# Loading half of the experts' late weight chunks through ScalarE's DMA queue

## The reference, cut to what matters

```python
def expert_ffn(xb, w1, b1, w2, b2):       # per expert: w1 [1024, 2048], w2 [1024, 1024]
    h = xb @ w1 + b1
    gate, up = h[:, :D_FF], h[:, D_FF:]
    gate = jnp.minimum(gate, SWIGLU_LIMIT)
    up = jnp.clip(up, -SWIGLU_LIMIT, SWIGLU_LIMIT)
    glu = gate * jax.nn.sigmoid(SWIGLU_ALPHA * gate)
    return ((up + 1.0) * glu) @ w2 + b2
```

## Time and profile before

| | us |
|---|---|
| median of 3 runs | 1476.92 |
| the profiled execution | 1473.57 |
| its span, as in the profile | 1471.8 |
| PE busy | 1367.5 (93%) |
| ACT busy | 233.6 (16%) |
| loads through the hardware queue q1 (SyncE), share of the 16 engines' time | 76.1% |
| granted TensorE clock, mean | 0.996 |

### The profile page before, as it was taken

One profiled execution on the slowest core, in us unless ns is written; L12 is line 12 of the kernel. 1 busy time (PEld: TensorE's weight loads), 2 busy tenths in 40 slices (PEclk: granted clock), 3 DMA queues, 4 the chain that ended last, 5 costly groups with the idle time before them and its releaser, 6 DMA issues.

```text
span 1471.8 us, 18292 instructions
## 1 busy us (share of the span) xinstructions
PE 1367.5 (93%) x7503; PEld 705.3 (48%) x7503; DVE 362.3 (25%) x671; ACT 233.6 (16%) x355; POOL 99.5 (7%) x167
## 2 busy tenths in 40 slices
PE   7999999999999989999889989899898898898987
PEld 6667668778888534433333233233332332332323
DVE  3224332532411242221212212212122122121222
ACT  1122232211000331111001111110011111100112
POOL 1022222220000210000000000000000000000000
PEclk9999999999999999999999999999999999999999
DMA  9787868775342459999999999999999999999995
GB/s 371 299 296 271 292 227 296 278 274 192 134 157 115 177 208 426 429 429 428 427 428 428 429 428 430 428 427 428 428 429 428 430 428 427 429 427 429 428 430 228
DMA packets 52321, 518.70 MB, mean 352 GB/s; under 512 B 6223, under 2 KB 6527, under 8 KB 19998
## 3 DMA queue, kind: packets, MB, share of 16 engines
q1 hardware_dynamic: 37418, 468.56, 76.1%
q0 software_dynamic: 12784, 45.34, 9.2%
q10 hardware_dynamic: 2084, 4.30, 0.8%
HBM read 496.55 MB, written 21.67 MB: 352 GB/s over the span
## 4 chain that ended last, share of the span: by engine, by line
DMA 53%; PE 43%; issue 1%; DVE 1%; ACT 1%; POOL 0%; SPq 0%; ACTq 0%; DVEq 0%; POOLq 0%
DMA ring<-in_w_pairs 46%; PE bank L1353 18%; PE bank L1644 11%; DMA out_ret_sample<-arena 5%; PE bank L1396 3%; PE bank L1683 2%; PE bank L1490 2%; PE bank L1593 1%; PE bank L1608 1%; PE bank L1455 1%; DMA k_kept<-arena 1%; PE bank L1444 0%; POOL arena L595 0%; DMA arena<-v_decode 0%; PE bank L1433 0%
## 5 line engine op out<-in xcount | busy, mean ns | idle before, releaser
L1644 PE MATMUL bank<-ring,arena 128*64 128x512 f32 x2048 | 461.0, 596 | 62.8 <-DMA ring<-in_w_pairs 61.3
L1353 PE MATMUL bank<-arena,ring 128*128 128x264 f32 x1536 | 349.5, 388 | 0.0
L1644 PEld LDWEIGHTS bank<-ring,arena 128*64 128x64 f32 x2048 | 141.4, 137 | 364.5 <-issue 273.3
L1353 PEld LDWEIGHTS bank<-arena,ring 128*128 128x128 f32 x1536 | 289.7, 190 | 53.2 <-issue 5.0
L1683 PE MATMUL bank<-ring,arena 128*64 128x512 f32 x1024 | 229.0, 595 | 11.5 <-DMA ring<-in_w_pairs 11.5
L1683 PEld LDWEIGHTS bank<-ring,arena 128*64 128x64 f32 x1024 | 70.9, 137 | 153.3 <-issue 124.9
L1305 DVE COPY arena<-bank 64x512 f32<-64x512 f32 x32 | 21.9, 684 | 237.5 <-PE bank L1683 237.5
L1283 DVE TENSOR_SCALAR arena<-bank 128x512 f32<-128x512 f32 x32 | 22.1, 692 | 231.8 <-PE bank L1644 231.8
L669 POOL CAST arena<-cst 128x128 bf16 x17 | 5.0, 296 | 907.9 <-PE bank L1672 907.9
L1608 PE MATMUL bank<-arena 128*128 128x512 f32 x136 | 62.9, 605 | 0.0
L1273 DVE TENSOR_TENSOR hs<-hs,bank 128x256 f32<-128x256 f32 x17 | 7.2, 421 | 223.7 <-PE bank L1604 223.7
(11 more groups left out here) (215 smaller groups left out, 850.3 us busy)
## 6 DMA issues: line engine op xcount, KB each, us to landing
ring<-in_w_pairs SPq DMA_DIRECT2D x192, 2048.0 KB, 24.4
ring<-in_w_mixer SPq DMA_DIRECT2D x60, 1024.0 KB, 9.8
arena<-in_state_ret POOLq DMA_DIRECT2D x32, 512.0 KB, 5.6
out_ret_sample<-arena POOLq DMA_DIRECT2D x32, 512.0 KB, 5.7
arena<-v_decode POOLq DMA_DIRECT2D x32, 256.0 KB, 8.4
out_ret_prompt<-arena ACTq DMA_DIRECT2D x4, 512.0 KB, 5.1
hx<-in_x_prompt SPq DMA_DIRECT2D x2, 512.0 KB, 3.7
v_kept<-arena ACTq DMA_DIRECT2D x2, 512.0 KB, 9.3
```

The source lines that it names most:

```text
L1353: ins = pe.matmul(bank[:, 0:T], weight(n + k // 4, k % 4)[:, 128 * j:128 * (j + 1)], rhs[:, k, :], start=k == 0, stop=k == KD * groups - 1)
L1644: ins = pe.matmul(out, xgT[:, k, 64 * e:64 * (e + 1)], held(n, 2 * D * (k % W1_KS) + c), start=False, stop=k == KD - 1)
```

## The change

Chunks 0 to 5 of each pair are loaded as before. Of chunks 6 to 11 SyncE loads partitions 0 to 63 only. Partitions 64 to 127 are loaded by ScalarE, in its own program: those of chunks 6 to 9 after the copy of L894, those of 10 and 11 after `low_half`. Each issue waits, as SyncE's does, for the slot's former chunk to have been used. Both halves raise the slot's semaphore by 16, so that PE now waits for 48 more per pair and slot instead of 32: 16 for the full chunk and 32 for the two halves.

```diff
+        def used(eng, it, n):          # as before, on any engine
+            ...
+        def expert_part(pair, n, lo, hi):
+
+            at = SLOT_CHUNKS * (n % WIDE_SLOTS)
+            return (ring[lo:hi, at:at + SLOT_CHUNKS, :].rearrange("p a n -> p (a n)"),
+                    w_pairs[bass.ds(pair, 1), n, lo:hi].rearrange("o p n -> p (o n)"))
...
             def load_pair(it, pair, first=False):
                 for n in range(PAIR_CHUNKS):
                     at = SLOT_CHUNKS * (n % WIDE_SLOTS)
-                    dst = ring[:, at:at + SLOT_CHUNKS, :].rearrange("p a n -> p (a n)")
-                    src = w_pairs[bass.ds(pair, 1), n].rearrange("o p n -> p (o n)")
...
+                    dst, src = expert_part(pair, n, 0, 64 if n >= WIDE_SLOTS else 128)
                     sp.dma_start(dst, src).then_inc(chunk[at], 16)
...
+            def second_halves(it, pair, chunks):
+
+                for n in chunks:
+                    used(ac, it, n - WIDE_SLOTS)
+                    dst, src = expert_part(pair, n, 64, 128)
+                    ac.dma_start(dst, src).then_inc(chunk[SLOT_CHUNKS * (n % WIDE_SLOTS)], 16)
...
                     ac.activation(pgT[:, 0:T], psum[TURN_BANKS[0]][:, 0:T], ACT.Copy).then_inc(pgT_ready, 1)
+                    second_halves(it, pair, range(6, 10))
                     for e in range(2):
...
                     low_half(r * GATHERS + pair + 1)
+                    second_halves(it, pair, range(10, 12))
...
                     def slot_ready(n):
 
-                        uses = PAIR_CHUNKS // WIDE_SLOTS
                         pe.wait_ge(chunk[SLOT_CHUNKS * (n % WIDE_SLOTS)],
-                                   16 * uses * it + 16 * (uses_before + n // WIDE_SLOTS + 1))
+                                   48 * it + 16 * uses_before + (48 if n >= WIDE_SLOTS else 16))
```

More of the change, by code:

```diff
@@ L492, in build @@
         w_mixer, w_pairs = a["w_mixer"], a["w_pairs"]
+        def used(eng, it, n):
+            if n < 2 * W1_CHUNKS:
+                e, part = divmod(n, W1_CHUNKS)
+                if part == W1_CHUNKS - 1:
+                    eng.wait_ge(up_done, 2 * it + (e + 1 + PRIMED))
+                else:
+                    eng.wait_ge(chunk_used, COUNTED * it + ((W1_CHUNKS - 1) * e + part + 1))
+            else:
+                e, part = divmod(n - 2 * W1_CHUNKS, W2_CHUNKS)
+                if part == W2_CHUNKS - 1:
+                    eng.wait_ge(down_done, 2 * it + (e + 1))
+                else:
+                    eng.wait_ge(chunk_used, COUNTED * it + (2 * (W1_CHUNKS - 1) + (W2_CHUNKS - 1) * e + part + 1))
+        def expert_part(pair, n, lo, hi):
+            at = SLOT_CHUNKS * (n % WIDE_SLOTS)
+            return (ring[lo:hi, at:at + SLOT_CHUNKS, :].rearrange("p a n -> p (a n)"),
+                    w_pairs[bass.ds(pair, 1), n, lo:hi].rearrange("o p n -> p (o n)"))
         @block.sync
@@ L523, in _ @@
                     load_tables(1 + n // 2)
[L525 to L538, removed]
             def load_pair(it, pair, first=False):
@@ L542, in load_pair @@
                     at = SLOT_CHUNKS * (n % WIDE_SLOTS)
-                    dst = ring[:, at:at + SLOT_CHUNKS, :].rearrange("p a n -> p (a n)")
-                    src = w_pairs[bass.ds(pair, 1), n].rearrange("o p n -> p (o n)")
                     if n >= WIDE_SLOTS:
-                        used(it, n - WIDE_SLOTS)
+                        used(sp, it, n - WIDE_SLOTS)
                     elif first:
@@ L550, in load_pair @@
                     else:
-                        used(it - 1, n + PAIR_CHUNKS - WIDE_SLOTS)
+                        used(sp, it - 1, n + PAIR_CHUNKS - WIDE_SLOTS)
+                    dst, src = expert_part(pair, n, 0, 64 if n >= WIDE_SLOTS else 128)
                     sp.dma_start(dst, src).then_inc(chunk[at], 16)
```

## The result

The changed kernel takes 1926.88 us (median of 4 runs, 1906.43 to 1953.09) against 1477.07: ratio 1.300 [1.294, 1.306], slower by 450 us. Predicted were 1622 us, in a range from 1480 to 1900. The sign was right, the size wrong by a factor of three, and the time lies outside the range, close to what rival (b) gave, 1944 us.

What follows compares the result with a forecast made beforehand. The prediction took DMA transfers to bound the kernel from about 541 us. It summed 1473.57 (profiled execution) + 7.8 (start of pair 1) + 141 (slower halves at factor 1.3) = 1622 us, range 1480 to 1900.

Steps and rivals of the forecast that it cites:

- rival (b): Late chunks of each pair: lower and upper halves serialise, factor 2.0, 470 us more, 1944 us; chance 0.21.
- The bound: Expert stage from about 541 us: DMA transfers bound the kernel, no idle DMA time in these 913 us.
- The start of pair 1: Pair 1, about 541.7 to 557.3 us: upper halves wait for L894's copy, missing transfers cost 7.8 us.
- ScalarE's halves are ready in time: Steady-state pairs: upper halves issued behind ScalarE's copies still start level with SyncE's halves; cost 0.
- Two queues cost nothing by themselves: Loads in flight on two queues: 423 GB/s pass at a share of 1.01, so factor 1.0.
- The half rate of one side: Narrow transfers, seen at 350.0 to 351.2 us: 209 GB/s for a full share against 424, factor 2.03.
- I take 1.3, between the wide row and 1.5: Late six chunks, both halves in flight: factor 1.3 on 29.4 us, 8.8 us per pair, 141 us in all.
- the wide row: Trace row with a POOL load and SyncE's ring loads, all on 128 partitions, at once: 423 GB/s, factor 1.0.
- The only narrow row: Trace row at 350.0 to 351.2 us, loads of `b_e1` and `b_e2` on 32 partitions each: factor 2.03.
- The range: Whole kernel's time: 1480 to 1900 us, since the factor was known only between two ends, 1.0 and 2.0.
- Rival (c): Late chunks: lower halves on some engines, upper on others, about 10 us idle per pair, 1640 us; chance 0.08.
- Rival (d): Expert stage: a second queue fills gaps between loads, faster; at 440 GB/s 1457 us; chance 0.04.

Runs made afterwards that it cites:

- even-odd kernel: Changed kernel with late chunks split into even partitions (SyncE) and odd ones (ScalarE) instead of lower and upper halves: 1484.39 us, 1.0046 of the kernel before.
- the 2 KB pieces: Changed kernel's lower and upper halves on two queues, each partition's 16 KB as eight 2 KB runs: late chunks only 1822.0 us, all 12 chunks 1676.6 us.
- one-sided stream alone: Changed kernel without ScalarE's calls, so partitions 64 to 127 of the late chunks are never loaded: 1621.0 us, 1.097 of the kernel before.

## Why the prediction was wrong

- *The bound* held: DMA share 1.0 before and after, and each microsecond of DMA time in the stage went to the end.
- *The start of pair 1*, 7.8 us: 8.3 in the even-odd kernel's stage, 1.1 once it was filled. Right. In the changed kernel it is not an addition of its own, since the lower halves at 206 GB/s leave no idle time (share 1.01), as rival (b) had it.
- *ScalarE's halves are ready in time*, cost 0: nearly. I put 2 us between its issue and the first data. By the packet records it was 3.8 us in the even-odd kernel and 6.7 in the changed one, where the lower halves went alone for about 7 us per pair. With even and odd partitions this cost nothing, as the other part went on at the full rate. The four issues took 2.61 us instead of 1.53.
- *Two queues cost nothing by themselves*: right, 428 GB/s with even and odd partitions, as the earlier trace rows had it with 423.
- *The half rate of one side*, 209 against 424 GB/s from 1.2 us of two small loads: right in size, 205 and 206 for halves alone. The row was misread, though: in its window `b_e1` had nearly gone, and 11 pieces of 8 KB, 41% of the bytes, belong to SyncE's ring load. What bears the half rate out is `b_e2`, whose 4 KB pieces took 0.31 us, twice a quarter of the 0.61 that 16 KB take.
- *"I take 1.3, between the wide row and 1.5"*: this is the step that failed, the factor for a lower and an upper half in flight together. The factor is 2.0, (88.2 - 29.4) / 29.4. It is worth 16 x 29.4 x 0.7 = 329 us, less the 7.8 that were counted twice; 1622 + 321 = 1943, against 1932.8 of the profiled execution. Both grounds were without a row: that engines hinder each other only when they meet on one side by chance (for 1.5), and that slack absorbs the turns (for less). With 16 KB pieces the records show neither: every piece is slow, in step or not. The only narrow row said 2.03, and nothing in the trace said that the other side's transfers bring it back. Why a piece is slow while other engines are on the opposite half stays open; the 2 KB pieces show only that their length matters.
- *The range* was cut at 1900, under the end of 1944 that the sum itself had given for the factor of 2.0. The ends of an unmeasured factor belong in the range.
- Rival (c), each half on engines of its own, is out: the lower halves alone keep a share of 0.99 to 1.01 busy. Rival (d) is out, 428 GB/s at best. Rival (b) had the serialising and the size; I gave it 0.21. Of its two ways, "all engines are on the same half together" is not what the records show, and "a collision costs both in full" comes nearer. The Trainium skill's rule behind it, in "DMA: Bandwidth & Descriptors", section "Rules for kernel authors" (two transfers to disjoint partition halves serialise), holds here with 16 KB pieces, at 236 GB/s against 206. With 2 KB pieces, at 348 to 372, it no longer does. The one-sided rate agrees with the Trainium skill's "SBUF — State Buffer", section "Door 1: The DMA port swizzle", by which partitions 0 to 63 reach only half of the ports: they moved at 205 GB/s against 428 for all 128. Partitions 32 to 95, on both sides, were fast: 90% of the 16 KB pieces in that kernel's stage took at most 0.62 us, and a third of them are the middle's.

## What to carry to other kernels

Don't cut a load of long pieces between partitions 63 and 64. If a load has to be split over queues, take even and odd partitions or columns, with pieces of the same size on all queues. When DMA share reads 1.0, read the GB/s beside it: a full share at half the rate was the mark of one-sided transfers here, and a second queue didn't cure it. Where the only row for an operation says factor 2, hold to it until another row says that something makes up for it.

## What was not expected of the hardware

- The engines take one piece (one contiguous run) of each queue in turn, so shares go by piece size: 8 KB beside 16 KB gave 141 to 286 GB/s, 2 KB beside 16 KB 39 to 44 to some 320.
- Smaller pieces cost rate with both sides in use: 428 GB/s at 16 KB, 422 at 8 KB, 387 at 2 KB (where the pieces also lie 256 bytes apart in HBM).
- In a one-sided stream alone the engines drifted apart after some 1000 us: 1621 us for three quarters of the bytes.
- ScalarE's issue of a half with 16 KB pieces took 0.48 us, and its data began to move 3.8 us after the issue with even and odd partitions, 6.7 us with the sides.
